# Attention softmax in a fused encoder block: VectorE divides tile t+1 before it takes the maximum of tile t+2

## The reference

```python
def attend(args):                       # one block b of 128 queries, all heads
    q_blk, b = args
    q_chunk = (b * 128 + jnp.arange(128)) // 64
    mask = key_chunk[None, :] <= q_chunk[:, None]
    s = jnp.einsum('bqhd,bkhd->bhqk', q_blk, k).astype(jnp.float32) * scale
    s = jnp.where(mask[None, None], s, neg)
    prob = jax.nn.softmax(s, axis=-1).astype(v.dtype)
    return jnp.einsum('bhqk,bkhe->bqhe', prob, v)
```

## Time and profile before

| what | value |
| --- | --- |
| median of three runs | 1249.42 us |
| profiled execution, its own time | 1250.04 us |
| its span (first to last instruction) | 1248.2 us |
| TensorE matmuls busy | 1235.0 us, 99% of the span |
| VectorE busy | 721.0 us, 58% |
| ScalarE busy | 483.3 us, 39% |
| GpSimd busy | 516.2 us, 41% |
| mean granted TensorE clock | 0.999 of full speed |

### The profile page before, as it was taken

The page is one execution under the profiler, slowest core; times in us unless marked ns, Lnnn a source line. Parts: engine busy times, 40 slices in busy tenths (PEclk is TensorE's granted clock), DMA queues, the critical chain, the costliest instruction groups (busy, mean ns, idle before and its releaser), DMA issues.

```text
span 1248.2 us, 16786 instructions
## 1 busy us (share of the span) xinstructions
PE 1235.0 (99%) x6014; PEld 1042.3 (84%) x6014; DVE 721.0 (58%) x1176; ACT 483.3 (39%) x892; POOL 516.2 (41%) x519
## 2 busy tenths in 40 slices
PE   9999999999999999999999999999999999999997
PEld 8888888888888888888888888888888888888886
DVE  5544444466664437855544455444489999954433
ACT  6622222256564224533333333333354344424422
POOL 3533443351110003555533455433499889810011
PEclk9999999999999999999999999999999999999999
DMA  9511101000021500242332342422554545420002
GB/s 342 166 34 42 44 2 43 1 10 26 17 92 62 152 1 1 76 127 93 118 114 70 113 127 85 127 85 85 185 192 160 171 169 187 150 85 1 1 34 101
DMA packets 101931, 115.09 MB, mean 92 GB/s; under 512 B 4832, under 2 KB 67680, under 8 KB 101856
## 3 DMA queue, kind: packets, MB, share of 16 engines
q1 hardware_dynamic: 101424, 113.57, 27.8%
q10 hardware_dynamic: 432, 0.54, 0.1%
HBM read 90.49 MB, written 23.59 MB: 91 GB/s over the span
## 4 chain that ended last, share of the span: by engine, by line
PE 95%; DVE 2%; ACT 1%; POOL 1%; issue 1%; DMA 0%; POOLq 0%; SPq 0%; DVEq 0%; ACTq 0%
PE PS L1738 11%; PE PS L1739 11%; PE PS L1737 11%; PE PS L208 8%; PE PS L206 8%; PE PS L207 8%; PE PS L2071 5%; PE PS L2073 5%; PE PS L2072 5%; PE PS L1032 3%; PE PS L1048 3%; PE PS L2450 2%; PE PS L2448 2%; PE PS L2449 2%; PE PS L2463 2%; PE PS L1039 1%
## 5 line engine op out<-in xcount | busy, mean ns | idle before, releaser
L206 PE MATMUL PS<-WF,HTH 128*128 128x512 f32 (+1 forms) x448 | 176.9, 395 | 0.5 <-DVE HTL L436 0.3
L208 PE MATMUL PS<-WF,HTL 128*128 128x512 f32 (+1 forms) x448 | 173.7, 388 | 0.0
L207 PE MATMUL PS<-WF,HTH 128*128 128x512 f32 (+1 forms) x448 | 173.3, 387 | 0.0
L1458 DVE TENSOR_TENSOR X<-X,PS 128x512 f32<-128x512 f32 x172 | 110.3, 679 | 53.4 <-PE PS L208 35.4
L1738 PE MATMUL PS<-HTL,WF 128*128 128x512 f32 x336 | 130.9, 389 | 0.0
L1737 PE MATMUL PS<-HTH,WF 128*128 128x512 f32 x336 | 130.9, 389 | 0.0
L1739 PE MATMUL PS<-HTH,WF 128*128 128x512 f32 x336 | 130.8, 389 | 0.0
L1670 DVE TENSOR_TENSOR WF<-RAW,WF 128x512 fp32r<-128x512 f32 x63 | 70.8, 1125 | 77.5 <-ACT WF L1660 77.5
L1739 PE MATMUL PS<-WF 128*128 128x512 f32 x252 | 98.1, 389 | 0.0
L1738 PE MATMUL PS<-WF 128*128 128x512 f32 x252 | 98.1, 389 | 0.0
L1737 PE MATMUL PS<-WF 128*128 128x512 f32 x252 | 98.1, 389 | 0.0
(11 more groups left out here) (266 smaller groups left out, 2814.4 us busy)
## 6 DMA issues: line engine op xcount, KB each, us to landing
hid<-TMP SPq DMA_DIRECT2D x74, 256.0 KB, 2.3
TMP<-hid SPq DMA_DIRECT2D x25, 512.0 KB, 4.5
RAW<-in_w_ffn_gate SPq DMA_DIRECT2D x22, 512.0 KB, 4.0
RAW<-in_w_ffn_up SPq DMA_DIRECT2D x22, 512.0 KB, 5.3
RAW<-in_w_ffn_down SPq DMA_DIRECT2D x22, 512.0 KB, 4.1
X<-in_x SPq DMA_DIRECT2D x16, 512.0 KB, 6.6
RAW<-in_w_in SPq DMA_DIRECT2D x32, 256.0 KB, 3.8
TAB<-hid SPq DMA_DIRECT2D x9, 512.0 KB, 4.5
```

Of the source, the lines that this page charges most:

```text
L206: nc.tensor.matmul(dst, HTH[:, k, tok], w_h, start=(k == 0), stop=False)
L207: nc.tensor.matmul(dst, HTH[:, k, tok], w_l, start=False, stop=False)
L208: last = nc.tensor.matmul(dst, HTL[:, k, tok], w_h, start=False, stop=(k == K - 1))
L1458: nc.vector.tensor_tensor(x, x, src, ALU.add).then_inc(done, 1)
```

## The change

In each step of a head VectorE does the same instructions with the same waits in another order: divide(t+1) comes first and biggest(t+2) behind it. The three steps ahead of the loop (biggest(0), biggest(1), divide(0)) stay, and so do the programs of all other engines. The function serves all four heads.

```diff
             biggest(1)
             divide(0)
             for t in range(T):
+                if t + 1 < T:
+                    divide(t + 1)
                 if t + 2 < T:
                     biggest(t + 2)
-                if t + 1 < T:
-                    divide(t + 1)
                 if turned and t == T - 1:
                     turned(1)
                 if t >= 1:
```

## The result

The changed kernel took 1253.4 us (median of seven runs, 1253.17 to 1254.26) against 1249.46 us (seven runs, 1249.25 to 1249.8): ratio 1.0034, 95% interval 1.0024 to 1.0043 (the quotient of the two medians is 1.0032, inside it). That is 3.9 us more, where 4.0 was forecast. The profiled execution has a span of 1252.4 us in place of 1248.2, 4.2 us more.

What follows compares the result with a forecast made beforehand. The prediction took TensorE to bound the kernel, with 95% of the span in its chain. Terms 0.79 + 0.22 = 1.01 us a head, times four 4.0 us, on 1249.42 gave 1253.4, rounded up to 1253.5; range 1252.2 to 1255.0 us.

Steps and rivals of the forecast that it cites:

- exp(2) lets go scores(4), and has no slack: In all four heads scores(4) starts 0.05 to 0.06 us behind exp(2)'s release; any delay of exp(2) delays TensorE.
- Term at scores(4): In each head scores(4) starts 0.79 us later, net of the earlier turn(1); bounds 0.6 to 1.0 us.
- Term at scores(5): In each head scores(5) waits for exp(3), 0.22 us more; bounds 0 to 0.4 us.
- Term at scores(6): In each head exp(4) is done 0.08 us before TensorE needs it, costing 0; bounds 0 to 0.3 us.
- The gain at turn(1) is swallowed: In head 1 turn(1) no longer waits for divide(1), saving 0.36 us, not kept because scores(4) comes next.
- Four heads alike: All heads have the same durations within 0.03 us and the same first two waits: 4 x 1.01 = 4.0 us.
- What a head loses goes to the end: Behind the heads TensorE has no slack, busy 738.77 of 739.00 us, so a head's loss reaches the end one to one.
- exp(7) in the last head: exp(7) comes some 1.2 us later, the turn of retention rows 1.0 us later; about 1 us of cover is left.
- a visible gap of 0.2 to 0.4 us before scores(5): Sign in the changed kernel's TensorE timeline: a second, smaller gap there, and none before scores(6) and (7).
- Not slower: Rival: only the earlier divide(1) counts for turn(1), 0.9 us less, 1248.5 us; chance 0.06.
- Half the price: Rival: scores(4) slips but scores(5) does not wait, 4 x 0.7 = 2.8 us, 1252.2 us; chance 0.12.
- The ring bounds every tile: Rival: serial exp, divide, biggest with 0.1 us longer handoffs delays scores(4) to (6), 6 us, 1255.4 us; chance 0.11.

Runs made afterwards that it cites:

- Step 0 alone: New order (divide(1) ahead of biggest(2)) only in the loop's step t = 0, old order in the others, against the kernel before: 1252.6 us, ratio 1.0027.
- steps 1 to 7 alone: Old order in the loop's step t = 0, new order from t = 1 on, against the kernel before: 1250.26 us, ratio 1.0008.
- Steps 2 to 7 alone: New order only from the loop's step t = 2 on (divide(3) ahead of biggest(4)), against the kernel before: 1249.23 us, ratio 1.0.
- the pad: Changed kernel with a waited-for 128x64 VectorE memset ahead of each maximum of tiles 2 to 7: 1255.2 us, ratio 1.005 against the kernel before.
- The kernel with the exchanged banks and step 0 alone: New order only at t = 0, PSUM banks of tiles 1 and 2 exchanged, scores(4) waiting for exp(1): 1248.41 us, ratio 0.9995 against the kernel before.
- its control: Kernel before, old order, with PSUM banks of tiles 1 and 2 exchanged and scores(4) waiting for exp(1): 1248.93 us, ratio 0.9998 against the kernel before.
- the exchange of banks in it: Changed kernel with PSUM banks of tiles 1 and 2 exchanged, scores(4) waiting for exp(1): 1253.42 us, ratio 1.0033 against the kernel before.

## Why the prediction was right

Point by point, by its own steps:

- *exp(2) lets go scores(4), and has no slack.* Right. The start follows the release by 0.05 to 0.06 us in both kernels; without that release scores(4) started 0.05 us sooner in the kernel before; and in the changed kernel 0.14 us more ahead of exp(2) come out as 0.14 us at scores(4).
- *Term at scores(4), 0.79 us.* Measured 0.79 in heads 0 to 2 and 0.78 in head 3. Step 0 alone brings it.
- *Term at scores(5), 0.22 us.* Measured 0.23, and 0.23 with steps 1 to 7 alone.
- *Term at scores(6), 0, with 0.08 us of slack.* exp(4) ended 0.14 us before the start and a release takes 0.05, so the slack was 0.09. Steps 2 to 7 alone cost 0.0 us; the pad used the slack up and showed 0.06 us there.
- *The gain at turn(1) is swallowed.* Right: turn(1) starts 0.33 us earlier in the head (0.36 was forecast), and nothing of it is left. The kernel with the exchanged banks and step 0 alone shows that a part of it can be had, 0.17 us against its control.
- *Four heads alike.* The prediction says that each head begins with the same two waits and has the same durations. Not so: turn(1) waits visibly in heads 1 and 2 only, and head 0 takes 28.17 us where head 1 takes 28.44. The sum does not suffer, since heads 0 to 2 lost 1.02, 1.06 and 1.09 us, and head 3 lost 1.06 up to its scores(7).
- *What a head loses goes to the end.* Right: these come to 4.2 us, the spans differ by 4.2 and the medians by 3.9. That the medians came within 0.1 us of the 4.0 is in part luck: the traces say 0.2 more than the sum, and the seven runs of the changed kernel lie 1.1 us apart.
- *exp(7) in the last head.* It was to come some 1.2 us later and leave about 1 us of cover for the turn behind it. It came 1.40 us later in the head and left 0.83 us (392.21 against 393.04), which still cost nothing.
- *What would show each step.* One sign was read wrongly beforehand: a visible gap of 0.2 to 0.4 us before scores(5). There is none, in any head. The wait is there by the starts, but it is hidden in the 0.2 us by which matmuls overlap. turn(2) ended 0.25 us behind the start of scores(5) before (318.87 and 318.62) and 0.02 us behind it now (320.66 and 320.64), which is the 0.23 us. The same overlap had been counted for turn(1) and forgotten for scores(5).
- *Rivals.* "Not slower" fell with the changed kernel and, in the form that blames the bank, with the exchange of banks in it. "Half the price" fell too, since scores(5) does wait; with step 0 alone it does not, and the loss is 3.1 to 3.4 us. "The ring bounds every tile" fell with steps 2 to 7. TensorE's granted clock was 1.00, its level of 2.4 GHz, from 283 to 405 us, with the new waits in it.
- *The rule of the Trainium skill* ("TensorE: Matmul & The Clock Gate", section "Architectural detail: the array is 16× 32×32, not 1× 128×128") that VectorE's queue is strictly first in, first out: the trace now agrees, with 18.2 us of waits before 28 divisions in the attention stage, and a ready maximum behind the first of them. The prediction held that the trace before says neither yes nor no; it agrees as well, with the ready divide(4) behind the waiting biggest(5).

Left open: why head 1 takes 0.02 us more behind scores(7) than at it, and whether the fastest kernel here, whose heads are shorter, is also faster as a whole, by the 0.06% of its median.

## What to carry to other kernels

Where an engine takes its instructions in order, as VectorE does here, look at what a waiting instruction holds up: putting a consumer of another engine's result ahead of that engine's next input turned two overlapped stages into one chain. It cost only where that chain was longer than TensorE's own step, for two of the tiles; from step 2 on the order made no difference. An engine that shows no idle time can still be let go by a release at the very moment it starts, so compare the start of each instruction with the end of what it waits for before calling a wait free. And a wait that is removed (here by other banks) pays only if what stands next in line is not as late.

## What was not expected of the hardware

A wait of up to about 0.2 us on TensorE leaves no idle time in the profile, since the records of successive matmuls, whose ends are modelled, overlap by that much. Longer waits are listed short by as much: scores(4) starts at 5.72 in the changed kernel and at 4.50 with the banks exchanged, 1.22 us apart, where the list has 0.98. In the changed kernel scores(5) lost 0.23 us in this way in head 1, and the list of TensorE's waits names only scores(4), with 3.4 us in four times. The sum of the listed new waits less those that went would have given 3.4 - 0.3 = 3.1 us, where the heads lost 4.2.
